# The level products of a chunk inverse, issued with 32 instead of 64 stationary columns

## The reference, cut to what matters

```
def step(S, inp):
    rt, wt, kt, vt, at, bt = inp
    sa = jnp.einsum('bhvk,bhk->bhv', S, at)
    S = S * wt[:, :, None, :] + sa[..., None] * bt[:, :, None, :] + vt[..., None] * kt[:, :, None, :]
    return S, jnp.einsum('bhvk,bhk->bhv', S, rt)
```

## Time and profile before

| | us |
|---|---|
| median of the runs | 2380.37 |
| span of the profiled execution | 2371.5 |
| first scan (layer 0), without its first 9 us | 197.9 |
| second scan (layer 1), without its first 9 us | 197.0 |

### The profile page before, as it was taken

How to read it: one execution, slowest core, us unless ns; L and a number is a source line. 1 busy time by engine, 2 the same in 40 slices (tenths; PEclk the granted TensorE clock), 3 DMA queues, 4 the chain that set the end, 5 groups by cost and what they waited for, 6 DMA issues and landing times. The chain is left out here.

```text
span 2371.5 us, 53901 instructions
## 1 busy us (share of the span) xinstructions
PE 2118.4 (89%) x23898; PEld 1360.0 (57%) x23898; DVE 720.8 (30%) x1768; ACT 487.9 (21%) x1120; POOL 275.6 (12%) x463
## 2 busy tenths in 40 slices
PE   6999899899899999999999689998898999986774
PEld 2454443899644444445556465555897887743443
DVE  1033435767431011310000023446775211300001
ACT  2123322333220000301111133323332302110001
POOL 0000000443100001101111200002442000011111
PEclk8999999899999999999999889997999999998886
DMA  7249825000122112639999811110001335799993
GB/s 284 71 156 344 285 93 195 3 4 5 55 89 94 66 66 99 237 104 379 386 384 384 295 53 48 63 49 2 4 4 50 140 133 209 262 380 379 384 382 124
DMA packets 183060, 399.91 MB, mean 169 GB/s; under 512 B 6672, under 2 KB 29072, under 8 KB 182640
## 3 DMA queue, kind: packets, MB, share of 16 engines
q1 hardware_dynamic: 170672, 361.94, 42.4%
q0 software_dynamic: 8576, 23.08, 2.6%
q10 hardware_dynamic: 3648, 12.45, 1.8%
HBM read 365.47 MB, written 31.98 MB: 168 GB/s over the span
## 5 line engine op out<-in xcount | busy, mean ns | idle before, releaser
L493 PE MATMUL ps<-H,memory 128*128 128x512 f32 (+2 forms) x1728 | 616.4, 513 | 12.3 <-DMA memory<-in_w_in 10.5
L493 PEld LDWEIGHTS ps<-H,memory 128*128 128x128 f32 (+1 forms) x1728 | 328.7, 191 | 287.7 <-issue 251.3
L730 PE MATMUL ps<-memory 64*64 64x32 f32 (+2 forms) x10112 | 333.4, 231 | 32.3 <-DVE memory L1623 10.3
L993 PE MATMUL ps<-memory 128*32 128x256 f32 x5120 | 307.5, 403 | 57.8 <-DMA memory<-in_eu 56.3
L730 PEld LDWEIGHTS ps<-memory 64*64 64x64 f32 x10112 | 321.1, 144 | 41.6 <-issue 19.7
L493 PE MATMUL ps<-memory 128*128 128x512 f32 (+3 forms) x928 | 319.8, 496 | 6.8 <-issue 3.0
L993 PEld LDWEIGHTS ps<-memory 128*32 128x32 f32 x5120 | 188.4, 116 | 174.2 <-issue 89.5
L493 PEld LDWEIGHTS ps<-memory 128*128 128x128 f32 (+1 forms) x928 | 173.7, 188 | 145.1 <-issue 127.5
L1018 PE MATMUL ps<-memory 128*32 128x256 f32 x2560 | 144.8, 380 | 4.9 <-ACT memory L1341 3.8
L1913 POOL TENSOR_TENSOR memory<-memory,cons 128x256 f32<-128x256 f32 x160 | 118.0, 753 | 122.8 <-DVE memory L1595 79.9
L1978 POOL DMA_DIRECT2D expert_rows<-memory x128 | 69.5, 543 | 436.9 <-DVE memory L1845 415.2
(11 more groups left out here) (251 smaller groups left out, 1807.1 us busy)
## 6 DMA issues: line engine op xcount, KB each, us to landing
memory<-in_eg SPq DMA_DIRECT2D x32, 2048.0 KB, 18.8
memory<-in_eu SPq DMA_DIRECT2D x32, 2048.0 KB, 24.6
memory<-in_ed SPq DMA_DIRECT2D x32, 2048.0 KB, 21.8
memory<-in_w_ada SPq DMA_DIRECT2D x24, 2048.0 KB, 10.4
memory<-in_w_in SPq DMA_DIRECT2D x20, 2048.0 KB, 8.2
expert_rows<-memory SPq DMA_DIRECT2D x4, 3456.0 KB, 23.6
memory<-in_w_out SPq DMA_DIRECT2D x4, 2048.0 KB, 7.9
memory<-expert_rows ACTq DMA_DIRECT2D x19, 384.0 KB, 6.9
```

Of the source, the lines that this page charges most:

```text
L493: ins = mm(ps[0:M, bank, 0:w], lhs(k), rhs(k), start=(k == 0), stop=(k == n - 1))
L730: ins = mm(out[cols, j], lhs[rows, j, :], rhs[rows, j], start=(n == 0), stop=(n == len(terms) - 1))
L993: ins = mm(out_.rearrange("p (x n) -> p x n", x=2), XGT[:, k, g * GROUP:g * GROUP + GROUP], sets[b][:, 0:2, k * 512 + c * P:k * 512 + c * ...
```

## The change

`heads` gets a width. In `join` and `grow` it is 32, so that each call becomes two, with stationary columns c to c+31 and output partitions to match; the moving operand, the sums and the semaphores stay. All other products keep 64.

```
+HALF = CH // 2
-                def heads(signal, *products):
+                def heads(signal, *products, width=CH):
...
                                 for h in range(2):
-                                    rows, cols = (slice(CH * (h ^ x), CH * (h ^ x) + CH) for x in (held, made))
-                                    ins = mm(out[cols, j], lhs[rows, j, :], rhs[rows, j], start=(n == 0),
-                                             stop=(n == len(terms) - 1))
+                                    rows = slice(CH * (h ^ held), CH * (h ^ held) + CH)
+                                    for c in range(0, CH, width):
+                                        cols = slice(CH * (h ^ made) + c, CH * (h ^ made) + c + width)
+                                        ins = mm(out[cols, j], lhs[rows, j, c:c + width], rhs[rows, j], start=(n == 0),
+                                                 stop=(n == len(terms) - 1))
...
-                    heads("joined", (under(part(d, 3, 0), n, d), (BTS[n][d], under(ONCE["X"][d], n, d), d, d)))
+                    heads("joined", (under(part(d, 3, 0), n, d), (BTS[n][d], under(ONCE["X"][d], n, d), d, d)), width=HALF)
...
-                        heads("grown", (under(part(d, 2, 1 - p), n, d), (TWICE["XT"][p][d], under(PS[n][d], n, d), d, d)))
+                        heads("grown", (under(part(d, 2, 1 - p), n, d), (TWICE["XT"][p][d], under(PS[n][d], n, d), d, d)), width=HALF)
...
-                        heads("grown", (under(part(d, 2, p), n, 1 - d), (PF[d], under(TWICE["XT"][p][d], n, 1 - d), d, d)))
+                        heads("grown", (under(part(d, 2, p), n, 1 - d), (PF[d], under(TWICE["XT"][p][d], n, 1 - d), d, d)), width=HALF)
```

## The result

The changed kernel takes 2501.94 us (median of 4 runs, 2494.76 to 2507.47), beside 2380.37 us for the kernel before on the same chip (3 runs, 2376.43 to 2385.64; a fourth run, of 2416.57 us, was in a slower state and is left out). The ratio is 1.0512, with a 95% interval of 1.0485 to 1.054. By that ratio the 2380.4 us of the start become 2502 us. The forecast was 2494, with 2405 to 2535 as its range.

The account below looks back on a forecast made before the run. TensorE's instruction supply was taken to bound the scans: 132 packets x 3.75 us = 495, plus 14 us of waits, 509 in place of 395, so +114. Added to 2380.4 this gave 2494 us, range 2405 to 2535.

Parts of the forecast that it names:

- Direction and size: Whole kernel: slower by 114 us, from 2380.4 to 2494 us, with bounds of +68 and +147.
- Instructions and packets: Level products in the scans: 5,120 more matmuls, 10,240 more rows with loads, so 132 instruction packets in place of 91.
- A packet's time: TensorE's instruction supply in the scans: 3.75 us a packet, 132 packets making 495 us; bounds 3.4 and 4.0 us.
- 14 us of waits at the borders of two steps: Between scan steps, TensorE waits for VectorE's last addition to the inverse: 0.84 us a step, 14 us for 16 steps.
- Between borders at least 1.2 to 1.3 plus 2.2 to 2.7 us: Scans: one packet border to the next takes at least 3.4 to 4.0 us, whatever the instructions cost.
- The 54 us of slack: Scans before the change: 54 us in which the supply isn't the limit, which the levels will use up.
- Credit for shorter loads nil: `join` and `grow` groups: narrower loads save 0 to 67 us, at most 34 credited, nil while packets are waited for.
- Changes of width, 240 in number: Scan steps: 240 switches between 64 and 32 columns at 0.15 us, 36 us, hidden inside the wait for packets.
- What would show it: Scans: packets 3.5 to 4 us apart, "issue" gaps at nearly every border, longer steps; projections and experts unchanged.
- the supply keeps up: Rival for the scans: no packet limit; 2416 us without gain on the array (0.08), 2382 with it (0.05).
- Faster: Rival for the scans: supply keeps up and width changes cost under 0.14 us, leaving the 34 us credit; 2346 us, 0.05.
- Slower supply: Rival for the scans: packets a fifth later once each is waited for, 4.5 us; +213, 2593 us, chance 0.07.

Follow-up runs that it names:

- e_all: Against the changed kernel, all products of the scan issued 32 columns wide, so no width changes inside it; 2670.22 us, ratio 1.1237.
- m_micro: Separate stream of small products only, without the kernel's work: groups of 64x64 or 64x32, unrolled and in loops; 298.74 us.
- e_join: Against the changed kernel, `grow` goes back to 64 columns, so only the `join` products are 32 wide; 2438.05 us, ratio 1.0261.
- e_grow: Against the changed kernel, `join` goes back to 64 columns, so only the `grow` products are 32 wide; 2427.16 us, ratio 1.0222.
- e_l4: Against the changed kernel, only the last of the five levels keeps 32 columns, the others go back to 64; 2396.85 us, ratio 1.0075.
- m_micro2: Separate stream of small products only, meant to repeat the unrolled 64x64 and 64x32 groups at full clock after warm-up loops; 464.69 us.
- e_split: Against the changed kernel, level products keep 64 stationary columns and are split by moving columns, 16 + 16 in place of 32; 2705.99 us, ratio 1.1367.
- m_micro4: Separate stream without the kernel's work: groups of small products with 96 already met waits, looped and unrolled, then unrolled pairs of widths; 458.27 us.

## Why the prediction was right, point by point

**Direction and size**: right. +122 us by the ratio, +128 on the profiled spans, against +114.

**Instructions and packets**: right. +5,120 matmuls and 132 packets in the scans, as worked out, 174 in all.

**A packet's time**: slightly low. The forecast took 3.75 us and called it the middle of 3.4 and 4.0, which is 3.7; with 3.7 the sum would have been +107. In `e_all`, where the supply limits nearly all of the scan, the scans' time by packet is 3.87, waits included; by that 132 packets come to 511 us, and the changed kernel's scans of 531 us leave 20 us for the waits and whatever else is not the supply, where the forecast had 495 and 14. Of the 22 us between 509 and 531, 13 are the windows that began late (395 for 408 us); the forecast of the difference was 9 us low.

**14 us of waits at the borders of two steps**: the place is right, the size too high. The changed kernel waits for this addition (L1626) 14 times, 7.5 us in all. There are other waits that the sum left out, 28.2 us for all engines, and since the kernel before has 29.7 they cancel.

**"Between borders at least 1.2 to 1.3 plus 2.2 to 2.7 us"**: held. The steady spacing of the streams is 3.45 us, at the low end of 3.4 to 4.0, with single ones to 4.01. The Trainium skill (Runtime: NRT & Kernel Launch, Instruction fetch mechanics) calls the cost of a block border mostly hidden. That holds in the streams' stretches of slow matmuls and in most of the kernel before; it doesn't hold in `m_micro`'s unrolled narrow groups, where each border shows 1.5 us or more, and the measurement decides.

**The 54 us of slack**: right that it is used up, but gradually. A packet more costs 2.2 us for the first 8 (by the runs 1.4 to 3.0), 2.5 for 20, 3.1 for 40 (123 us) and 3.5 for each of the 49 from there to `e_all`. Only at the end of that row does the rate near the supply's full 3.45 to 3.87. The forecast took this full rate for all 132 packets of the changed kernel and set the slack against it, which comes to 2.8 us for each added packet and so near the 3.1; for a smaller change the marginal costs are the better price.

**Credit for shorter loads nil**: right for this kernel, for the reason given. The array does gain. A `join` group of 32 matmuls lies between 517.23 and 517.61, 0.38 us with its changes of width, against 0.43, and the loop has 0.33 against 0.46. I had said under 0.3 us, which no row shows. What is gained is waited away at the next border.

**Changes of width, 240 in number**: counted right. The price was too high: about 0.10 us from the loops, not 0.15. Hidden in the waits, as said: the 124 more of them in `e_join` than in `e_grow` show in TensorE's busy time (9.4 us more) and not in the length of the scans.

**What would show it**: a step takes 531.1 / 16 = 33.2 us (said: 31 to 33, so just outside; before 25.5 over the same extent), VectorE's share of the scans is 277.1 of 531.1 us, 52% (said: about 54%), gaps of 0.4 to 1.9 us in the step shown (said: 0.5 to 1.5). The loads of 64x32 show 119 ns in the mean of the changed kernel and 112 in `m_micro`'s narrow loop (said: 110). Only the scans changed: outside them the span is 1968.8 us, before 1963.4; the other kernels of this study scatter around that (`e_join` 1971.2, `e_grow` 1959.9, `e_l4` 1969.5) in no relation to their edit.

**What the forecast left out**: the granted clock in the scans fell from 0.94 to 0.85 and from 0.87 to 0.79. Idle gaps and a lower clock come together here. Where a block's work is shorter than the wait for the next the clock adds nothing, as `m_micro2` shows for a block and `e_all` for whole scans (3.82 and 3.80 us). In the changed kernel packets lie 3.88 us apart at the full clock (64 times) and 4.03 at 1.2 GHz (22 times). An estimate from the traces: had the stretches at 1.2 GHz gone at the pace of the others (28.8 ns a matmul, before 32.5), the scans would be 52 us shorter, and those before 34 us; so the clock has at most some 17 of the 123 us, within the 20 us that TensorE is busy longer.

**The rivals**: "the supply keeps up" is refuted, since by it the change would have cost 36 us, 48 with its highest price of a width change. "Faster" had a true premise, a width change under 0.14 us and shorter work, and fell because the supply doesn't keep up. "Slower supply" did not come: 3.87 us, not 4.5.

## What to carry to other kernels

No stream or scan here had unrolled matmuls and loads pass TensorE faster than 3.5 to 3.9 us in the mean for 256 instructions, some 14 to 15 ns each, or 27 to 30 ns for a matmul with its load, at either level of the clock. Products of 64x32 on four tiles, which the array passes at 10.2 ns, are held by that long before they are by the array; those of 64x64 on two tiles, at 28.6 ns, sit right at the border. Before splitting a product to shorten loads or to use more tiles, count instruction packets in the stretch and divide: if it already runs near 4 us a packet, every packet more cost 2.2 to 3.5 us here, whether the array gained or not. In a loop small enough to stay fetched (up to 1,536 instructions in the stream) narrow products do pay; no run tried that in the kernel. And look at the granted clock of each stretch, not only at the count: `e_split` issues as many instructions as the change and costs some 200 us more.

## What the runs showed of the hardware that was not expected

- In a loop that fits, matmuls of 64x32 with their loads on four tiles go at 10.2 ns each (984 in 10 us), against 28.6 ns (350 in 10 us) for 64 columns on two tiles: half the columns, under three quarters of the time for the same product.
- TensorE kept six blocks of 256 instructions through the passes of a loop, but ahead of straight code it never had more than the next block.
- A stream can be dense and stay at the slow pace. `m_micro` has 1276 wide matmuls on two tiles between 2 and 71 us, 54 ns each; `m_micro2` and `m_micro4` go on like this for over 120 us, and in `m_micro2` the clock stays at 0.50 through the 280 us from 178 us on, dense throughout and mostly of this form. The rise to the full level on record comes in `m_micro` at 130.8 us, 5 us into the dense loop of narrow products on four tiles (from 14.2 to 10.2 ns each), and again at 243.5 us, in the second dense loop of them; then wide products on two tiles, too, go at 28.6 ns for 33 us. Why is open.
- A granted clock of 1.00 can mean that the trace has no record of it; the pace of a known form (28.6 or 53 ns for the wide one) tells the level.
- A met wait on TensorE's queue costs 92 to 99 ns at the slow pace: in the stream a group with 48 of them takes 5.25 to 5.6 us where one without takes 0.85. Of equal waits written one after the other only half appear in the profile and in the packets (20 more of 40).
- Twice the instructions on two tiles (`e_split`) cost 13.7%, on four tiles 5.1%: the dense two-tile form ran at a granted clock of 0.65 and 0.60 in the scans, the four-tile form, with its gaps, at 0.85 and 0.79. `e_all`, at 0.67 and 0.67, costs less than `e_split` with 49 packets more, since the lower clock falls into its waits.
